# Sample attention with the cached values as the stationary operand and one batch row's probabilities as eight moving columns

## The reference, cut to what matters

```python
DEC_BATCH = 8; DEC_SEQ = 8; N_MEM = 256; N_XHEADS = 4; XHEAD_DIM = 256
def cross_attend(h, k, v, w_q, w_o):
    q = (h @ w_q).reshape(Bn, L, N_XHEADS, XHEAD_DIM)
    s = jnp.einsum('blhd,bmhd->bhlm', q, k).astype(jnp.float32) * (XHEAD_DIM ** -0.5)
    p = jax.nn.softmax(s, axis=-1).astype(v.dtype)
    o = jnp.einsum('bhlm,bmhd->blhd', p, v).reshape(Bn, L, D_MODEL)
    return o @ w_o
```

## Time and profile before

| what | us |
|---|---|
| median of 3 runs | 2263.92 |
| lowest and highest run | 2262.98, 2266.09 |
| profiled execution, its own time | 2266.19 |
| its span from first to last instruction | 2264.5 |
| mean granted TensorE clock of the span | 0.993 of full |

### The profile page before, as it was taken

How to read it: one execution, slowest core, us unless ns; L and a number is a source line. 1 busy time by engine, 2 the same in 40 slices (tenths; PEclk the granted TensorE clock), 3 DMA queues, 4 the chain that set the end, 5 groups by cost and what they waited for, 6 DMA issues and landing times.

```text
span 2264.5 us, 34688 instructions
## 1 busy us (share of the span) xinstructions
PE 2184.0 (96%) x14272; PEld 2122.4 (94%) x14272; DVE 1235.3 (55%) x1417; ACT 597.3 (26%) x947; POOL 825.7 (36%) x599
## 2 busy tenths in 40 slices
PE   6999999999999999999999999998999999899997
PEld 5998899999999999999999986798999999899997
DVE  5558899653121222213454363269988885764763
ACT  5331222122101010111111172014333333333334
POOL 6114100004444434443454402146544444544541
PEclk9999999999999999999999999999999999999999
DMA  6422332123212112111311304321444347645322
GB/s 210 144 80 84 123 118 96 61 84 100 66 56 67 57 57 67 47 47 46 118 45 47 102 20 167 122 86 58 158 158 149 122 143 275 234 155 159 119 70 79
DMA packets 220344, 237.59 MB, mean 105 GB/s; under 512 B 8120, under 2 KB 181176, under 8 KB 218151
## 3 DMA queue, kind: packets, MB, share of 16 engines
q1 hardware_dynamic: 201814, 203.17, 27.7%
q10 hardware_dynamic: 18145, 32.57, 4.1%
q0 software_dynamic: 256, 0.01, 0.0%
HBM read 177.53 MB, written 58.67 MB: 104 GB/s over the span
## 4 chain that ended last, share of the span: by engine, by line
PE 88%; DVE 6%; DMA 2%; ACT 1%; issue 1%; POOL 0%; ACTq 0%; SPq 0%; DVEq 0%; POOLq 0%
PE PS L1055 52%; PE PS L1494 13%; PE PS L1541 13%; PE PS L1404 1%; PE PS L1442 1%; DMA raw_A<-in_w_ff 1%; DVE opnd L2662 1%; DVE slots_d L2226 1%; PE PS L1375 1%; PE PS L1124 1%; PE PS L1086 1%; PE PS L1360 1%; PE PS L1417 1%; DVE w_lo L2249 1%; DMA x_res<-x_scratch 0%
## 5 line engine op out<-in xcount | busy, mean ns | idle before, releaser
L892 POOL TENSOR_TENSOR w_hi<-w_raw,ones 128x512 fp32r<-128x512 f32 x150 | 175.9, 1173 | 801.0 <-PE PS L1055 755.8
L1541 PE MATMUL PS<-opnd,slot 128*128 128x272 f32 x2688 | 343.8, 290 | 9.7 <-POOL slot L957 4.8
L1541 PEld LDWEIGHTS PS<-opnd,slot 128*128 128x128 f32 x2688 | 341.2, 190 | 10.8 <-DVE opnd L2662 3.1
L1494 PE MATMUL PS<-opnd,slot 128*128 128x272 f32 x2688 | 340.1, 288 | 6.7 <-DVE opnd L2662 3.1
L1494 PEld LDWEIGHTS PS<-opnd,slot 128*128 128x128 f32 x2688 | 338.1, 188 | 8.4 <-issue 4.6
L1055 PE MATMUL PS<-h_hi,w_hi 128*128 128x364 f32 x1512 | 337.1, 331 | 6.1 <-DVE w_lo L2249 5.8
L1055 PE MATMUL PS<-h_lo,w_hi 128*128 128x364 f32 x1512 | 334.1, 329 | 0.0
L1055 PE MATMUL PS<-h_hi,w_lo 128*128 128x364 f32 x1512 | 333.8, 329 | 0.0
L957 POOL TENSOR_TENSOR slot<-raw_A,slot 128x512 fp32r<-128x512 f32 x160 | 241.0, 1512 | 246.7 <-ACT slot L1554 246.3
L2497 DVE TENSOR_TENSOR tmp<-PS,tmp 128x728 f32<-128x728 f32 x64 | 43.4, 720 | 431.3 <-PE PS L1055 431.3
L1055 PEld LDWEIGHTS PS<-h_hi,w_hi 128*128 128x128 f32 x1512 | 260.6, 188 | 12.0 <-issue 10.2
(11 more groups left out here) (323 smaller groups left out, 3105.9 us busy)
## 6 DMA issues: line engine op xcount, KB each, us to landing
w_raw<-in_w_in SPq DMA_DIRECT2D x64, 512.0 KB, 4.0
hid_scratch<-stage SPq DMA_DIRECT2D x16, 1904.0 KB, 6.6
opnd<-hid_scratch SPq DMA_DIRECT2D x56, 544.0 KB, 5.9
raw_A<-in_w_ff SPq DMA_DIRECT2D x64, 256.0 KB, 3.1
raw_A<-in_w_ff SPq DMA_DIRECT2D x32, 512.0 KB, 5.0
branch_scratch<-oring ACTq DMA_DIRECT2D x16, 544.0 KB, 2.9
xring<-in_x_prompt SPq DMA_DIRECT2D x16, 512.0 KB, 4.9
w_raw<-in_w_branch SPq DMA_DIRECT2D x16, 512.0 KB, 3.5
```

The lines of the kernel that those rows point to most:

```text
L892: nc.gpsimd.tensor_tensor(w_hi[:, z % 2, cols], w_raw[:, z % 2, cols], ones[:, 0:1].broadcast_to([P, 512]), ALU.mult).then_inc(w_hi_done, 1)
L1494: mm = mmul(product_of(u, p)[:, c, :], w, x[:, HC * c:HC * c + HC], start=(j == 0 and e == 0), stop=(j == PAIRS - 1 and e == 2))
L1541: mm = mmul(product2_of(t)[:, c, :], w, x[:, part, HC * c:HC * c + HC], start=(j == 0 and e == 0), stop=(j == 2 * PAIRS - 1 and e == 2))
```

## The change

The operands of the value product change places. What is held is now a 128x128 piece of the cached values, and what moves is the eight columns of `pt_s` that belong to the batch row. For each batch row there are 4 heads, 2 halves of the head's channels (`dt`) and 2 halves of the memory, 16 matmuls, and 128 over all. The result stands with channels on partitions, all of it in bank 4, in the order in which `mv_hi` wants it. So the transposes back (step 6), the copy to `p_s` before them, and the waits on `so_copied` and `so_t` are gone. `pt_s` has no zeros: POOL's memset goes, and DVE makes one copy of 512 columns in place of eight of 64. DVE now waits itself for `pv_ready` 16 (the prompt's attention, whose `v_hi` shares the memory).

```diff
-    ptm = at("ptm", [P, DEC_B, 2 * HEADS * N_SAMPLE], Q[1] + 49152)
+    pt_s = at("pt_s", [P, 2 * HEADS, N_SAMPLE], Q[1] + 49152)
...
-        pool.wait_ge(pv_ready, 16)
-        nc.gpsimd.memset(ptm[:, :, :], 0.0).then_inc(ptm_zero, 1)
...
             for h in range(HEADS):
-                for mt in range(MT):
-                    j = 2 * h + mt
-                    v0 = mt * D_MODEL + h * HEAD_DIM
-                    mm = mmul(PS[0:N_SAMPLE, 4 + h, 0:HEAD_DIM], ptm[:, b, j * N_SAMPLE:(j + 1) * N_SAMPLE],
-                              kvring[:, n % 4, v0:v0 + HEAD_DIM], start=(b == 0 and mt == 0),
-                              stop=(b == 7 and mt == 1))
+                for dt in range(2):
+                    o0 = (2 * h + dt) * N_SAMPLE + DEC_L * b
+                    for mt in range(MT):
+                        v0 = mt * D_MODEL + h * HEAD_DIM + dt * P
+                        mm = mmul(PS[:, 4, o0:o0 + DEC_L], kvring[:, n % 4, v0:v0 + P],
+                                  pt_s[:, 2 * h + mt, DEC_L * b:DEC_L * (b + 1)], start=(mt == 0), stop=(mt == 1))
             mm.then_inc(so_ready, 1)
         product_chunk(N_XO, S_XO, 1, mv_hi, mv_lo)
-        pe.wait_ge(so_copied, 1)
-        for kt in range(KT):
-            mm = tr(PS[:, 3, kt * N_SAMPLE:(kt + 1) * N_SAMPLE], p_s[:, kt * P:(kt + 1) * P],
-                    ident[0:N_SAMPLE, 0:N_SAMPLE])
-        mm.then_inc(so_t, 1)
...
         act.wait_ge(so_ready, DEC_B)
-        copy(p_s[:, :].rearrange("p (h d) -> p h d", h=HEADS), PS[0:N_SAMPLE, 4:8, 0:HEAD_DIM]).then_inc(so_copied, 1)
-        act.wait_ge(so_t, 1)
-        copy(mv_hi[:, :, SEQ:T], PS[:, 3, :].rearrange("p (k t) -> p k t", k=KT)).then_inc(so_hi, 1)
+        copy(mv_hi[:, :, SEQ:T], PS[:, 4, :].rearrange("p (k t) -> p k t", k=KT)).then_inc(so_hi, 1)
...
-        dve.wait_ge(ptm_zero, 1)
-        blocks = PS[:, 3, :].rearrange("p (j t) -> p j t", t=n64)
-        for b in range(DEC_B):
-            ins = v.tensor_copy(ptm[:, b, :].rearrange("p (j t) -> p j t", t=n64)[:, :, DEC_L * b:DEC_L * (b + 1)],
-                                blocks[:, :, DEC_L * b:DEC_L * (b + 1)])
-        ins.then_inc(sm_pt, 1)
+        dve.wait_ge(pv_ready, 16)
+        v.tensor_copy(flat(pt_s[:, :, :]), PS[:, 3, :]).then_inc(sm_pt, 1)
```

More of the change, by code:

```diff
@@ L534, in _build @@
         S("pt_lo_done"), S("pv_ready"), S("o_hi"), S("o_lo"))
-    qm_zero, ptm_zero = S("qm_zero"), S("ptm_zero")
+    qm_zero = S("qm_zero")
     qm_ready, ks_t, ss_ready = S("qm_ready"), S("ks_t"), S("ss_ready")
-    sm_mx, sm_e, sm_p, sm_t, sm_pt, so_ready, so_copied, so_t, so_hi, so_lo = (
-        S("sm_mx"), S("sm_e"), S("sm_p"), S("sm_t"), S("sm_pt"), S("so_ready"), S("so_copied"), S("so_t"),
-        S("so_hi"), S("so_lo"))
+    sm_mx, sm_e, sm_p, sm_t, sm_pt, so_ready, so_hi, so_lo = (
+        S("sm_mx"), S("sm_e"), S("sm_p"), S("sm_t"), S("sm_pt"), S("so_ready"), S("so_hi"), S("so_lo"))
     x2_out = S("x2_out")
@@ L2650, in _ @@
         dve.wait_ge(sm_t, 1)
-        dve.wait_ge(ptm_zero, 1)
-        blocks = PS[:, 3, :].rearrange("p (j t) -> p j t", t=n64)
-        for b in range(DEC_B):
-            ins = v.tensor_copy(ptm[:, b, :].rearrange("p (j t) -> p j t", t=n64)[:, :, DEC_L * b:DEC_L * (b + 1)],
-                                blocks[:, :, DEC_L * b:DEC_L * (b + 1)])
-        ins.then_inc(sm_pt, 1)
+        dve.wait_ge(pv_ready, 16)
+        v.tensor_copy(flat(pt_s[:, :, :]), PS[:, 3, :]).then_inc(sm_pt, 1)
         dve.wait_ge(so_hi, 1)
-        v.tensor_tensor(mv_lo[:, :, SEQ:T], PS[:, 3, :].rearrange("p (k t) -> p k t", k=KT),
+        v.tensor_tensor(mv_lo[:, :, SEQ:T], PS[:, 4, :].rearrange("p (k t) -> p k t", k=KT),
                         mv_hi[:, :, SEQ:T].bitcast(F32), ALU.subtract).then_inc(so_lo, 1)
```

## The result

The changed kernel takes 2292.43 us (median of 4 runs, 2291.04 to 2293.82), the kernel before beside it 2263.45 us: a ratio of 1.0129 with a 95% interval of [1.0117, 1.014]. That is 29.0 us more, where 23.4 were forecast (2287); it lies 0.4 us above the upper end of the stated range, 2259 to 2292. The profiled execution took 2291.65 us, with a span of 2289.9 us.

What follows compares the result with a forecast made beforehand. TensorE, busy 96% of the span, was taken as the bound. Waits, copies and full-clock product -2.2, clock fall +23.6, recovery +2.0 gave +23.4 us: 2289.6 on the profiled execution, 2287 on the median, range 2259 to 2292.

Steps and rivals of the forecast that it cites:

- hand-over and copies: Transposes and copies between projection chunks 1 and 2 go, 2.1 us; DVE's single copy saves 0.5; together 2.6 us.
- value product: 256 load-matmul pairs replace 27.8 us: +0.4 at full clock, +23.6 more as the clock falls, 51.8 us in all.
- recovery of the clock: Projection behind the product starts at the low clock for 4.5 us, 15 matmuls, costing +2.0 us.
- POOL's removed wait: POOL's memset and wait, 50 us upstream: removal gives nothing, since POOL then waits 37.3 us for TensorE.
- The pair at full clock: In the value product, one load of 128 columns plus its narrow matmul takes 0.11 us, set by the load.
- the dear pair: Rival for the value product: clock holds but loads aren't hidden, 0.15 us per pair, 2272 us; chance 0.06.
- the quick load: Rival for the value product: clock holds, loads take 0.07 us as for the transposes, 2251 us; chance 0.08.
- the page's rule of some 60 cycles: Skill page's cost for any matmul up to 60 columns; by it alone 256 pairs take an estimated 6.4 us.
- The clock: TensorE's clock falls to the 1.2 GHz level in the value product because loads stream nearly nothing; chance 0.60.
- the time of the fall: Clock falls 3 us after the product's start, bounds 0.5 and 6; 27 pairs quick, 229 at 0.213 us.
- The step's upper bound, +26.1: Value product's extra time if the clock falls 0.5 us after the product's start: +26.1 us.
- The rival that the clock holds because TensorE is never without work: In the value product, the load sets the pace at 0.103 to 0.12 us, 2261.7 us; chance 0.26.

Runs made afterwards that it cites:

- second comparison: Changed kernel run again, 2291.95 us, beside the same with POOL's wait for pv_ready put back, 2288.87 us; the kernel before took 2263.45 us.
- experiment 4: Kernel before with operands exchanged, 64 masked columns moving, chunk 1 spread 12, 6 and 6 matmuls into the gaps and behind the product; 2259.96 us, ratio 0.9979.
- experiment 5: Kernel before, product and hand-over untouched, only chunk 1 of the projection spread 12, 6 and 6 matmuls; 2259.2 us, ratio 0.9982.
- experiment 2: Kernel before with only the operands exchanged, all 64 columns of the masked tile moving, gaps unfilled; 2290.75 us, ratio 1.0115.
- 7: Kernel before, unchanged, traced twice more; 2267.07 and 2264.13 us, one execution each.
- 8: Kernel before with DVE's eight copies made twice, a longer gap before the value product; 2267.41 us, ratio 1.0016.
- experiment 3: Changed kernel with POOL's wait put back and chunk 1 moved into the two gaps ahead of the product, 12 matmuls each; 2281.93 us, ratio 1.0074.
- experiment 9: Kernel before with operands exchanged, 32 masked columns moving, chunk 1 spread 12, 6 and 6 matmuls; 2281.81 us, ratio 1.0081.
- experiment 6: Changed kernel with the second 128 keys of every batch row left out, 128 pairs in place of 256; 2265.92 us.

## Why the prediction was wrong in its size and right in its main mechanism

| Term, us | forecast | measured | from |
|---|---|---|---|
| hand-over and copies | -2.6 | -2.6 | -2.14 and -0.44, the two chains |
| value product | +24.0 | +26.8 | 27.82 to 54.60, start to chunk 1's start |
| recovery of the clock | +2.0 | +1.5 | 5.59 - 4.08 |
| POOL's removed wait | 0 | +3.1 | medians of the changed kernel with and without it |
| sum | +23.4 | +28.8 | medians: +29.0, and +28.5 in the second comparison |

**The hand-over** went as worked out: ACT's 0.60 and DVE's 0.69 lie beside chunk 1, and chunk 2 follows without a gap. DVE's copy of 512 columns took 0.70 in place of the 0.65 assumed, at the edge of its bounds.

**The pair at full clock** was forecast at 0.11 and is 0.111 with 8 and 32 columns and 0.112 with 64. At full clock the product is 1.0 us longer with the exchange (28.78 in experiment 4) than without (27.81 in experiment 5), where the prediction had 0.4. The rivals of the dear pair (0.15) and the quick load (0.07) are ruled out by those rows. So is the page's rule of some 60 cycles for a matmul of up to 60 columns, in "TensorEngine Tiling (Array Packing)", section "Instruction Overhead" of the Trainium skill, as a price for pairs with a load: the prediction's estimate by it was 6.4 us, and 256 pairs took 28.8 at full clock.

**The clock** fell, as forecast with 0.60, and the pair at the low level took 0.214 for the 0.213 assumed. **The term that was mis-sized is the time of the fall.** The step let it come 3 us after the product's start, with 27 quick pairs in that time, and had 0.5 as the earliest. It came at the product's start or before it, so all 256 pairs ran low: 54.75 us for 51.8. (The step's upper bound, +26.1, comes to +25.9 when its own terms are added again; against the same 28.2 us, 54.60 is +26.4.) The reason lies in a sentence ahead of that step, that the waits around the transposes "didn't lower it". One execution had been read as a rule; in two of three the same gaps lower the clock in the kernel before as well, and there the wide product hides that, at 1.4 us. The change does two things to the clock, and the prediction held only the second: the product no longer lifts the clock that the gaps had lowered (the changed kernel and experiment 2, against 7 and 8), and it lowers one that is up (experiment 3). The 3 us would have fitted an entry without gaps, where the fall came 5 us in with 8 columns and 2.6 with 32. With the gaps filled and POOL's wait in place the second alone still leaves it 18 us over the kernel before (2281.93 and 2264.0). So the larger part of the loss, which the prediction did have, doesn't depend on the gaps.

The rival that the clock holds because TensorE is never without work had 0.26. In experiments 3 and 9 the clock falls with loads and matmuls following without a gap. The Trainium skill, "TensorE: Matmul & The Clock Gate", section "The HAM clock gate", names an idle window as what lowers the clock; if idle means an engine without instructions, these runs contradict it, and the measurement decides.

**The recovery**, 4.5 us in the prediction with 3.6 and 6 as its bounds, took 3.4 us in the first trace of the changed kernel, just under the lower bound, and 5.9 us in the second and in experiment 6. Its price varied with it, 1.5 us in the first trace and 2.6 in the second; that the table's 1.5 lies so near the forecast's 2.0 is partly luck of the trace.

**POOL's wait** is the step that failed outright, a term put at nothing that measured 3.1 us. The prediction's third removal, the memset, "costs nothing before and gives nothing now", because POOL has 37.3 us to spare behind it. That looked at whether POOL would be late and not at whom an earlier POOL would meet. With the wait gone POOL's four splits start beside DVE's masked queries, DVE needs 2.8 us more, and TensorE's clock is down behind the longer gap of 4.37 us. This term and the product's extra 2.8 us together carry the time past 2292; either alone would have left it inside the range. "SBUF — State Buffer", section "Who interferes with whom", of the Trainium skill says that a DVE instruction with two inputs in this memory contends with a POOL instruction that reads it, not with one that only writes it. The rows agree: the queries have two inputs, beside splits they take up to 1280 ns, about the length of a split (1.26), and 220 ns without; DVE's next two instructions, `mv_lo<-PS,mv_hi` with one of their two inputs in PSUM, lie beside a split too and take 1.27 us together, as against 1.28 without. POOL's memset, which only writes, isn't beside the queries in either kernel, so that half of the rule is not shown here. The prediction had the order of POOL's list and could have asked this of it.

**Left open.** That the terms add up to 28.8, so near the 29.0 of the medians, is partly luck. The product's +26.8 is against the trace without the fall; against the other two executions it is +25.4. In the profiled pair the upstream stretch, from POOL's memset of `qm` to the second group of key transposes (L1417 before, L1414 after), grew by 5.4 us and not 3.1, and it differs by 4.3 between the two kernels of the second comparison. Other stretches give some of it back, and not by their clock: from the first matmul of the next stage (L1494 before, L1486 after) to the end, the profiled pair took 725.4 and 722.1 us, with the low level in about 17 us of either. But the two further traces of the kernel before took 722.7 and 725.2 there, so a spread of some 3 us is in that stage without any change; its cause was not looked for. No width between 32 and 64 columns was run, and whether the values matter was not tested either: 24 of the 32 columns in experiment 9 and 56 of the 64 in experiment 4 are zeros.

## What to carry to other kernels

Before making the moving operand narrow, price the pair of load and matmul by the load, and then by the load at half clock: with full loads, 8 or 32 columns ran at 1.2 GHz for the rest of the stretch while TensorE was busy in all of each window, and only the clock's column shows it. Gaps ahead of a narrow stretch can cost more than their own length: with 64 columns the same product took 54.8 us behind gaps and 28.8 without them. Fill them with wide work; that was worth 4 us to the kernel before without any other change. And when an edit removes a wait on an engine with time to spare, look at which instructions that engine will now run, and beside whom.

## What the runs showed of the hardware that was not expected

- A stretch of loads of 128 columns, each followed by a matmul of few moving float32 columns, entered at the high clock: with 64 columns it held for 28.8 us; with 32 it fell 2.6 us in, with 8 5 us in (experiments 4, 9, 3). Entered at the low clock: 64 columns stayed low for 54.8 us (experiment 2); 256 columns past a held operand of 64 had it back 2.8 to 5.5 us after the start (experiments 7, 8).
- The pair cost 0.111 to 0.112 us at the high level with 8, 32 and 64 columns, and 0.214 at the low level with 8 and 64.
- Four DVE instructions of 64 columns with both inputs in SBUF took 3.39 us beside POOL's splits and 0.63 without.
- The same two gaps, 2.0 and 1.3 us, lowered the clock in two of three executions of the kernel before.
